# Seven half products for each gate and value panel of the first FFN, and both FFNs' inner dimension in quarters

## The chip, the cores and the metric

One core of one Trainium2 chip runs the whole program. The metric is device time in microseconds (us), the median of three runs. TensorE multiplies, ScalarE (ACT) and VectorE (DVE) do elementwise work, GpSimd (POOL) helps them, SyncE (SP) issues the loads of weights.

## The reference

Two transformer blocks with a second network behind them; the change touches the FFN of each of the two blocks (everything is float32):

```python
def swiglu(x, w_in, w_out):
    a, g = jnp.split(x @ w_in, 2, axis=-1)
    return (jax.nn.silu(a) * g) @ w_out
...
    xn = rms_norm(x, g2) * (1 + scale2) + shift2
    return x + gate2 * swiglu(xn, w_fi, w_fo)
```

`w_fi` is 1024 x 5632 (22 chunks of 128 gate columns and 22 of 128 value columns), `w_fo` is 2816 x 1024. The first block (l = 0) works on 768 tokens (512 and 256 of context), the second (l = 1) on 512. `shift`, `scale` and `gate` come from a product of `w_mod` with a conditioning vector: 96 chunks of 128 rows, the modulation chunks.

## The kernel before, in words

Activations stand with features on the partitions and tokens in the free dimension. A weight matrix is cut into panels of 128 output features; `plan()` lists them in the order in which TensorE takes them, and a panel has a running number j. A panel's product is exact to float32 by three passes of a reduced-precision format (fp32r): weight and operand are each split into a high and a low half, and high x high, high x low and low x high are added in PSUM (`panel`, L578 to L594, the matmul is L592). A panel of the first FFN's `fin` has 8 chunks x 3 passes x 2 token segments (512 and 256) = 48 matmuls, one of its `fout` 11 x 6 = 66. Results go to one of two PSUM banks in turn (`BANK`).

For panel j: SP loads it into a ring of four buffers (waiting until the low half of the panel four places before is made), ScalarE copies it to `whi` (`high`, L1132) once the panel two before is done, GpSimd subtracts to make `wlo` (L571), TensorE waits for `lo_ready`. An FFN is cut in halves: `fin{l}{half}` has 11 gate and 11 value panels in turn, `fout{l}{half}` takes the 11 hidden chunks. After a gate panel ScalarE writes silu of the bank into `fsilu` (L1424). After a value panel VectorE multiplies (`fh`, L2063, this frees the bank), ScalarE copies that to `hidden_hi` (L1429) and VectorE subtracts for `hidden_lo` (L2066, semaphore `h_lo`), which the first panel of `fout` waits for chunk by chunk. `gated_add` (L1766) adds a `fout` panel times its gate to the residual. Between these VectorE works off modulation chunks 40 to 95, one for each panel (`own_mod`, two operations over 1024 columns each, L1737), all through one buffer `modw4`: SP loads chunk k when chunk k - 1 has been worked off.

Each engine's queue is written out by hand and is executed in order; engines meet only through semaphores. While the second block's fin10 runs, VectorE also computes angles for a later stage, and ScalarE takes their sines after panel 19 of 22 (L1421). Before each norm TensorE is given some idle products (`keep_busy`, L648).

## Time and profile before

| | |
|---|---|
| median of three runs | 2265.54 us (2264.86 to 2266.88) |
| the profiled execution's own time | 2265.63 us |
| its span, first to last instruction | 2263.5 us |
| mean granted TensorE clock | 0.988 |
| busy: TensorE, VectorE, ScalarE, GpSimd | 2195.1, 1174.5, 732.7, 631.1 us |
| weight loads of TensorE (beside its matmuls) | 1775.7 us |
| matmuls | 11148 |

The profile is one execution. Busy time of an engine is the sum over its instructions; a matmul's recorded length reaches past the start of the next, so TensorE's rate is read from start to start.

### The profile page before, as it was taken

Reading aid. Unit: us, or ns where it says so; the run is one execution under the profiler, and the core shown is the slowest. Engines: PE = TensorE matmul, PEld = TensorE weight load, DVE = VectorE, ACT = ScalarE, POOL = GpSimd, SP = SyncE. Lnnn points to the kernel's source line nnn. Section 1 sums busy time; section 2 is a strip of 40 time slices with the busy share of each in tenths; the row PEclk is TensorE's granted clock in tenths of the full one; section 3 lists DMA queues with packets and bytes.
Section 4 is the critical chain, followed back from the end, with each engine's and each line's share of the span. In section 5 each row is a group of like instructions: output and inputs, shape, how many; then the busy total and the mean of one; then the engine's idle time right before and its main releaser. Section 6 shows DMA issues by size and latency. Waiting matters only on the chain.

```text
span 2263.5 us, 26814 instructions
## 1 busy us (share of the span) xinstructions
PE 2195.1 (97%) x11148; PEld 1775.7 (78%) x11148; DVE 1174.5 (52%) x1533; ACT 732.7 (32%) x1101; POOL 631.1 (28%) x272
## 2 busy tenths in 40 slices
PE   8998899999999999999999999999999999999998
PEld 6884588888888888785678888887788888888756
DVE  5987677656556665696454212347232344432172
ACT  4323424221112121424543222222263222334652
POOL 0000003223332233200144434443224444423402
PEclk9999999999999999999999999999999999989999
DMA  7302231333333342211023323323212333311301
GB/s 306 119 21 101 75 135 62 131 129 130 104 112 126 118 149 83 79 47 75 28 82 101 108 85 96 114 72 93 84 60 90 97 99 93 93 56 53 98 23 56
DMA packets 59592, 214.14 MB, mean 95 GB/s; under 512 B 6608, under 2 KB 10320, under 8 KB 58320
## 3 DMA queue, kind: packets, MB, share of 16 engines
q1 hardware_dynamic: 57024, 206.57, 27.4%
q10 hardware_dynamic: 2448, 5.85, 0.8%
q8 instruction: 89, 1.46, 0.3%
q14 instruction: 31, 0.25, 0.0%
HBM read 210.30 MB, written 2.10 MB: 94 GB/s over the span
## 4 chain that ended last, share of the span: by engine, by line
PE 89%; DVE 6%; ACT 3%; issue 1%; POOL 1%; DMA 0%; POOLq 0%; ACTq 0%; DVEq 0%
PE prod L592 74%; PE misc L638 2%; PE prod L727 1%; PE prod L807 1%; PE prod L775 1%; PE prod L862 1%; PE misc L1038 1%; PE misc L714 1%; DVE conv_acc L1941 1%; PE prod L691 1%; PE misc L886 1%; DVE stat L1872 1%; PE misc L682 1%; PE misc L874 1%; PE prod L656 1%
## 5 line engine op out<-in xcount | busy, mean ns | idle before, releaser
L571 POOL TENSOR_TENSOR wlo<-ring,whi 128x1024 fp32r<-128x1024 f32 (+3 forms) x252 | 599.4, 2379 | 1579.3 <-ACT whi L1132 1579.3
L592 PE MATMUL prod<-operand_hi,whi 128*128 128x512 f32 (+1 forms) x2080 | 769.5, 370 | 12.3 <-POOL operand_lo L558 4.6
L592 PE MATMUL prod<-operand_lo,whi 128*128 128x512 f32 (+1 forms) x2080 | 759.1, 365 | 0.0
L592 PE MATMUL prod<-operand_hi,wlo 128*128 128x512 f32 (+1 forms) x2080 | 755.6, 363 | 0.0
L1132 ACT ACTIVATE whi<-ring 128x1024 fp32r<-128x1024 f32 (+3 forms) x278 | 287.3, 1034 | 709.5 <-PE prod L592 688.1
L592 PEld LDWEIGHTS prod<-operand_hi,whi 128*128 128x128 f32 x2080 | 393.4, 189 | 90.8 <-issue 11.5
L592 PEld LDWEIGHTS prod<-operand_hi,wlo 128*128 128x128 f32 x2080 | 392.2, 189 | 64.8
L592 PEld LDWEIGHTS prod<-operand_lo,whi 128*128 128x128 f32 x2080 | 393.1, 189 | 62.9 <-issue 3.1
L592 PE MATMUL prod<-hidden_lo,whi 128*128 128x512 f32 (+1 forms) x528 | 188.0, 356 | 0.0
L592 PE MATMUL prod<-hidden_hi,whi 128*128 128x512 f32 (+1 forms) x528 | 187.6, 355 | 0.0
L592 PE MATMUL prod<-hidden_hi,wlo 128*128 128x512 f32 (+1 forms) x528 | 186.6, 353 | 0.0
L1737 DVE CUSTOM_DVE_ANT_0 mod_junk<-modw,silu_c,par 128x1024 bf16<-128x1024 f32 x68 | 121.4, 1786 | 78.8 <-DMA modw<-in_wmod 78.2
L1766 DVE SCALAR_TENSOR_TENSOR resid<-prod,par,resid 128x512 f32<-128x512 f32 x72 | 45.4, 658 | 178.2 <-PE prod L592 178.2
L2066 DVE TENSOR_TENSOR hidden_lo<-ffn_h,hidden_hi 128x768 fp32r<-128x768 f32 (+1 forms) x44 | 112.3, 2552 | 42.6 <-ACT hidden_hi L1429 42.6
L1737 DVE CUSTOM_DVE_ANT_0 modw<-modw,silu_c,par 128x1024 f32<-128x1024 f32 x68 | 132.5, 1948 | 0.0
L2063 DVE TENSOR_TENSOR ffn_h<-ffn_silu,prod 128x768 f32<-128x768 f32 (+1 forms) x44 | 36.1, 820 | 179.9 <-PE prod L592 179.9
L592 PEld LDWEIGHTS prod<-hidden_hi,whi 128*128 128x128 f32 x528 | 99.6, 189 | 15.5 <-POOL wlo L571 0.5
L592 PEld LDWEIGHTS prod<-hidden_hi,wlo 128*128 128x128 f32 x528 | 99.3, 188 | 14.7
L592 PEld LDWEIGHTS prod<-hidden_lo,whi 128*128 128x128 f32 x528 | 99.5, 188 | 13.7
L1941 DVE SCALAR_TENSOR_TENSOR conv_acc<-glu,par,conv_acc 128x798 f32<-128x798 f32 (+1 forms) x120 | 104.5, 913 | 1.3
L1424 ACT ACTIVATE ffn_silu<-prod 128x768 f32<-128x768 f32 (+1 forms) x44 | 31.0, 706 | 225.6 <-PE prod L592 225.6
L1343 ACT ACTIVATE probs_t<-misc 128x512 f32<-128x512 f32 x52 | 30.9, 595 | 66.4 <-PE misc L874 66.4
(316 smaller groups left out, 2412.1 us busy)
## 6 DMA issues: line engine op xcount, KB each, us to landing
ring<-in_w SPq DMA_DIRECT2D x224, 512.0 KB, 3.6
modw<-in_wmod SPq DMA_DIRECT2D x68, 512.0 KB, 3.6
ring<-in_w SPq DMA_DIRECT2D x32, 704.0 KB, 4.8
mod_pair<-in_wpair SPq DMA_DIRECT2D x8, 1024.0 KB, 16.8
ring<-in_wmod SPq DMA_DIRECT2D x12, 512.0 KB, 4.6
dft<-in_dftx SPq DMA_DIRECT2D x8, 512.0 KB, 5.1
resid<-in_xt SPq DMA_DIRECT2D x4, 768.0 KB, 7.6
ring<-in_w SPq DMA_DIRECT2D x12, 192.0 KB, 2.3
```

Of the source, the lines that this page charges most:

```text
L571: nc.gpsimd.tensor_tensor(wlo_of(j)[:, 0:w], ring[PLACE["panel", j] % RING][:, 0:w], whi_of(j)[:, 0:w].bitcast(F32), ALU.subtract).then_in ...
L592: mm = pe.matmul(G[b][:, t0:t0 + tn], w[:, k * P:(k + 1) * P], a[:, t0:t0 + tn], start=(i == 0 and q == 0), stop=(i == g.kc - 1 and q == 2))
L638: mm = pe.matmul(out[:, h * tb:h * tb + h], square[:, t:t + P], sel, start=(c == 0 and tb == 0), stop=(c == nchunks - 1 and tb == nb - 1), ...
L656: mm = pe.transpose(M0[:, tb * P:(tb + 1) * P], r[:, tb * P:(tb + 1) * P], ident)
L1132: nc.scalar.activation(whi_of(j)[:, 0:w], ring[PLACE["panel", j] % RING][:, 0:w], ACT.Copy).then_inc(hi_ready, 1)
L1343: nc.scalar.activation(probs_t[at % 3][:, :], M1[:, :], ACT.Copy).then_inc(pair_copied, 1)
L1424: nc.scalar.activation(fsilu[:, 0:width], src[:, 0:width], ACT.Silu).then_inc(free, 1)
L1737: nc.vector.tensor_tensor_reduce((junk, w)[s][:, 0:DC * P], w[:, 0:DC * P], silu_c[:, 1024 * s:1024 * (s + 1)], 1.0, col, ALU.mult, ALU.ad ...
L1766: ins = nc.vector.scalar_tensor_tensor(X[:, p, t0:t0 + tn], G[b][:, t0:t0 + tn], pa(f"mod{l}")[:, col:col + 1], X[:, p, t0:t0 + tn], ALU.m ...
L1941: ins = nc.vector.scalar_tensor_tensor(o, glu[:, c, tap:tap + wide], w, o, ALU.mult, ALU.add)
L2063: nc.vector.tensor_tensor(fh[:, 0:width], fsilu[:, 0:width], G[b][:, 0:width], ALU.mult).then_inc(bank_free[b], 1)
L2066: nc.vector.tensor_tensor(HL[:, p // 2, 0:width], fh[:, 0:width], HH[:, p // 2, 0:width].bitcast(F32), ALU.subtract).then_inc(h_lo, 1)
```

## The change

In the first block's FFN, after the first four panels, a gate panel and its value panel together make a unit. The 256 weight columns x 1024 features are seen as a 2 x 2 matrix of blocks (gate or value; first or second half of the features), the operand as a 2 x 2 matrix (features by halves; tokens by halves of 384), and the four result blocks come from seven products of sums of blocks (Strassen's scheme in Winograd's form) in place of eight. Each product is 4 chunks x 3 passes of 384 columns. The operand's sums are made once (`operand_sums`, `operand_sum`), the weights' sums for each unit on VectorE (`weight_sums`, `last_weight_sum`); each of the seven weight factors is split again, high on ScalarE (`half_weights`), low on VectorE for four sums (`sum_low`) and on GpSimd for the three plain blocks (`block_lows`). The results are put together in four other PSUM banks, a to d, and by VectorE's `product_sum`. Both FFNs take their 22 hidden chunks in quarters of 6, 5, 6, 5, so that there are four `fin` and four `fout` stages each and `fout` adds to the residual four times. Ring and weight buffers shrink from 11 to 8 chunks; there is one modulation chunk for each unit and for each `fout` panel, eight chunks (88 to 95, buffer `modw5`) move to the second block's `fin10`, panels 4 to 11; the angles move to `fin11`, its sines to its last panel (9). In panels whose name doesn't begin with f, the passes are the outer loop and the two token segments the inner.

The diff, cut to its core (`NTH[j]` is the number of panels up to j that are computed as before):

```diff
+PLAIN_FIRST = 4
+HALVED = {g.j0 + p for g in GEMMS if g.name[:4] == "fin0" for p in range(PLAIN_FIRST if g.name == "fin00" else 0, g.n)}
...
+def mod_places():
+    at = [GEMM["fin00"].j0 + p for p in (1, 3)]
+    for q in range(4):
+        at += [unit_panel(q, u) for u in units_of(q)]
+        at += [GEMM[f"fout0{q}"].j0 + p for p in range(8 if q < 3 else 2)]
+    return at + [GEMM["fin10"].j0 + p for p in range(4, 12)]
+MOD_AT = mod_places()
+assert len(MOD_AT) == MOD_ALL - MOD_WOUT
...
+        def weight_slot(w, q, i):
+            s, b = (i + (q > 0)) % 4, GEMM["fin00"].j0 % 2
+            return w[b if s < 2 else 1 - b][:, 512 * (s % 2):512 * (s % 2) + 512]
...
+        UB4 = M0[:, 0:HN], M0[:, 512:512 + HN], M1[:, 0:HN], MM[:, 0:HN]
...
+                if kind == "panel" and i in HALVED:
+                    q = next(q for q in range(4) if i < GEMM[f"fout0{q}"].j0)
+                    u = units_of(q)[0] + (i - unit_panel(q, units_of(q)[0])) // 2
+                    odd = (i - GEMM["fin00"].j0) % 2
+                    sp.wait_ge(w_lo, 3 * u + 2 + odd)
+                    sp.wait_ge(sum_lo, 4 * u + (1 if odd else 4))
...
-                elif j > GEMM["wout0"].j0 + 10 and own + 1 < MOD_ALL:
+                elif j == GEMM["fin00"].j0 + 3 or j - 4 in MOD_AT[:-1]:
...
+            def block_lows(q, j):
+                first = units_of(q)[0]
+                u = first + (j - unit_panel(q, first)) // 2
+                for of, at_, idx in ((0, 0, 0), (0, 512, 3), (1, 512, 6)):
+                    i = 7 * (u - first) + idx
+                    pool.wait_ge(w_hi, 7 * u + idx + 1)
+                    nc.gpsimd.tensor_tensor(weight_slot(wlo, q, i), ring[PLACE["panel", j + of] % RING][:, at_:at_ + 512],
+                                            weight_slot(whi, q, i).bitcast(F32), ALU.subtract).then_inc(w_lo, 1)
...
+                    both = [(s, x) for s in segs for x in passes] if name[0] == "f" else [(s, x) for x in passes for s in segs]
...
+            def halves(q):
+                a, b, c, d = UB4
+                first, second = slice(0, HN), slice(HN, NT)
+                steps = ((a, (XH[:, 0:4, first], XL[:, 0:4, first])), (c, (TH[1], TL[1])), (a, (TH[0], TL[0])),
+                         (b, (XH[:, 4:8, first], XL[:, 4:8, first])), (a, (XH[:, 0:4, second], XL[:, 0:4, second])),
+                         (d, (XH[:, 4:8, second], XL[:, 4:8, second])), (c, (TH[2], TL[2])))
+                for u in units_of(q):
+                    i0 = 7 * (u - units_of(q)[0])
+                    for idx, (bank, (high, low)) in enumerate(steps):
+                        if idx in (0, 3, 6):
+                            pe.wait_ge(w_lo, 3 * u + idx // 3 + 1)
+                        else:
+                            pe.wait_ge(sum_lo, 4 * u + {1: 1, 2: 2, 4: 3, 5: 4}[idx])
+                        if u == 0 and idx in (1, 2, 4, 6):
+                            pe.wait_ge(t_lo, {1: 1, 2: 2, 4: 3, 6: 4}[idx])
+                        if idx == 0:
+                            wait(pe, unit_copied, 3 * u)
+                        elif idx == 1:
+                            wait(pe, unit_sum, 4 * u)
+                        elif idx == 2:
+                            pe.wait_ge(unit_copied, 3 * u + 1)
+                        elif idx == 4:
+                            pe.wait_ge(unit_copied, 3 * u + 2)
+                        elif idx == 6:
+                            pe.wait_ge(unit_sum, 4 * u + 2)
+                        wh, wl = weight_slot(whi, q, i0 + idx), weight_slot(wlo, q, i0 + idx)
+                        for k in range(4):
+                            for t, (w, x) in enumerate(((wh, high), (wh, low), (wl, high))):
+                                mm = pe.matmul(bank, w[:, k * P:(k + 1) * P], x[:, k, :], start=(idx in (0, 1, 3, 5) and k == 0 and t == 0),
+                                               stop=(k == 3 and t == 2), skip_group_check=True)
+                        mm.then_inc(unit_done, 1)
...
                 big(f"wout{l}", xh, xl, width, begin=2)
                 rms(1, width, W, total=W[1])
-                for half in range(2):
-                    big(f"fin{l}{half}", xh, xl, width, ready=OPS[f"fin{l}0"])
-                    big(f"fout{l}{half}", lambda k: HH[:, k, :], lambda k: HL[:, k, :], width, hidden=FH * (2 * l + half + 1))
+                for q in range(4):
+                    if l or q == 0:
+                        big(f"fin{l}{q}", xh, xl, width, ready=OPS[f"fin{l}0"], panels=None if l else PLAIN_FIRST)
+                    if l == 0:
+                        halves(q)
+                    big(f"fout{l}{q}", lambda k: HH[:, k, :], lambda k: HL[:, k, :], width, hidden=CHUNKS[l, q])
...
+            def half_weights(q, i):
+                first = units_of(q)[0]
+                u, idx = first + i // 7, i % 7
+                j = unit_panel(q, u)
+                if i >= 4:
+                    act.wait_ge(unit_done, 7 * first + i - 3)
+                elif q == 0:
+                    act.wait_ge(panel_done, NTH[GEMM["fin00"].j0 + (0, 0, 3, 3)[i]])
+                else:
+                    act.wait_ge(panel_done, NTH[GEMM[f"fout0{q - 1}"].j0 + (6, 7, 7, 6)[i]])
+                gate, value = (ring[PLACE["panel", j + s] % RING] for s in range(2))
+                if idx in (0, 3, 6):
+                    landed(act, ("panel", j + (idx == 6)))
+                else:
+                    act.wait_ge(w_sum, 4 * u + {4: 1, 1: 2, 2: 3, 5: 4}[idx])
+                src = (gate[:, 0:512], value[:, 0:512], S2t[:, :], gate[:, 512:1024], S1t[:, :], gate[:, 512:1024], value[:, 512:1024])[idx]
+                nc.scalar.activation(weight_slot(whi, q, i), src, ACT.Copy).then_inc(w_hi, 1)
...
+                def hidden_half(u, half):
+                    act.wait_ge(half_ready, 2 * u + (2 if half == 0 else 1))
+                    nc.scalar.activation(HH[:, unit_chunk(q, u), HN * half:HN * half + HN], (U2t, C22t)[half][:, :],
+                                         ACT.Copy).then_inc(half_hi, 1)
+                for u in units_of(q):
+                    i0 = 7 * (u - first)
+                    for idx in range(7):
+                        act.wait_ge(unit_done, 7 * u + idx + 1)
+                        if idx == 0:
+                            wait(act, half_ready, 2 * u - 2)
+                            nc.scalar.activation(P1t[u % 2][:, :], a, ACT.Copy).then_inc(unit_copied, 1)
+                        elif idx == 2:
+                            wait(act, h_lo, CHUNKS[0, q] + unit_chunk(q, u))
+                            nc.scalar.activation(U2t[:, :], a, ACT.Copy).then_inc(unit_copied, 1)
+                        elif idx == 4:
+                            nc.scalar.activation(U4t[:, :], a, ACT.Copy).then_inc(unit_copied, 1)
+                        if i0 + idx + 4 < count:
+                            half_weights(q, i0 + idx + 4)
+                        if i0 + idx == free:
+                            high(fout)
+                        if i0 + idx == count - 1:
+                            high(fout + 1)
+                        if idx == 0 and u > first:
+                            hidden_half(u - 1, 0)
+                        elif idx == 3:
+                            act.wait_ge(unit_sum, 4 * u + 1)
+                            nc.scalar.activation(P1t[u % 2][:, :], P1t[u % 2][:, :], ACT.Silu).then_inc(unit_silu, 1)
+                        elif idx == 5:
+                            act.wait_ge(unit_sum, 4 * u + 3)
+                            nc.scalar.activation(U4t[:, :], U4t[:, :], ACT.Silu).then_inc(unit_silu, 1)
+                        elif idx == 6:
+                            hidden_half(u, 1)
+                hidden_half(u, 0)
...
+                        if g.name == "fin00" and p == 3:
+                            half_weights(0, 2)
...
+                        if g.name == "fin00" and p == 1:
+                            act.wait_ge(t_sum, 4)
+                            operand_sum(TH[1], UA[:, :, HN:NT])
+                            operand_sum(TH[0], UB[:, :, HN:NT])
+                            half_weights(0, 0)
+                            half_weights(0, 1)
+                        elif g.name == "fin00" and p == 3:
+                            half_weights(0, 3)
+                            operand_sum(XH[:, 0:4, HN:NT], UA[:, :, 0:HN])
+                            operand_sum(TH[2], UB[:, :, 0:HN])
...
+                    def next_weights(p, q=q):
+                        if p == 6:
+                            half_weights(q + 1, 0)
+                        elif p == 7:
+                            for i in (1, 2, 3):
+                                half_weights(q + 1, i)
...
+            def operand_sums():
+                dve.wait_ge(odd_lo, DC // 2)
+                dve.wait_ge(operand_lo, n["op"])
+                for U, c in ((UA, 0), (UB, 4)):
+                    ins = nc.vector.tensor_tensor(U[:, :, :], XH[:, c:c + 4, :].bitcast(F32), XL[:, c:c + 4, :].bitcast(F32), ALU.add)
+                link(ins)
+                A, B, one, two = UA, UB, slice(0, HN), slice(HN, NT)
+                for k, (o, x, y) in enumerate(((A[:, :, one], A[:, :, two], A[:, :, one]), (A[:, :, two], B[:, :, two], A[:, :, two]),
+                                               (B[:, :, two], B[:, :, two], A[:, :, one]), (B[:, :, one], B[:, :, one], B[:, :, two]))):
+                    nc.vector.tensor_tensor(o, x, y, ALU.subtract).then_inc(t_sum, 1)
+                    dve.wait_ge(t_sum, k + 1)
...
+            def weight_sums(q, u):
+                A11, _, A21, A22 = raw(q, u)
+                landed(dve, ("panel", unit_panel(q, u)))
+                landed(dve, ("panel", unit_panel(q, u) + 1))
+                wait(dve, sum_lo, 4 * (u - 1) + 3)
+                nc.vector.tensor_tensor(S1t[:, :], A21, A22, ALU.add).then_inc(w_sum, 1)
+                dve.wait_ge(w_sum, 4 * u + 1)
+                nc.vector.tensor_tensor(A21, A11, A21, ALU.subtract).then_inc(w_sum, 1)
+                nc.vector.tensor_tensor(S2t[:, :], S1t[:, :], A11, ALU.subtract).then_inc(w_sum, 1)
+            def last_weight_sum(q, u):
+                _, A12, _, _ = raw(q, u)
+                dve.wait_ge(w_lo, 3 * u + 2)
+                dve.wait_ge(w_sum, 4 * u + 3)
+                nc.vector.tensor_tensor(A12, A12, S2t[:, :], ALU.subtract).then_inc(w_sum, 1)
+            def sum_low(q, i):
+                u, idx = units_of(q)[0] + i // 7, i % 7
+                _, A12, A21, _ = raw(q, u)
...
+            def halves(q):
+                a, b, c, d = UB4
+                for u in units_of(q):
+                    i, more, k = 7 * (u - units_of(q)[0]), u < units_of(q)[-1], unit_chunk(q, u)
+                    def product_sum(which, done, copied, out, x, bank):
+                        dve.wait_ge(unit_done, 7 * u + done)
+                        dve.wait_ge(unit_copied, 3 * u + copied)
+                        nc.vector.tensor_tensor(out[:, :], x[:, :], bank, ALU.add).then_inc(unit_sum, 1)
...
+                        dve.wait_ge(unit_silu, 2 * u + silu)
+                        dve.wait_ge(unit_sum, 4 * u + (2, 4)[order])
+                        nc.vector.tensor_tensor(value[:, :], value[:, :], gate[:, :], ALU.mult).then_inc(half_ready, 1)
+                        dve.wait_ge(half_ready, 2 * u + order + 1)
+                        dve.wait_ge(half_hi, 2 * u + order + 1)
+                        o = slice(HN * half, HN * half + HN)
+                        return nc.vector.tensor_tensor(HL[:, k, o], value[:, :], HH[:, k, o].bitcast(F32), ALU.subtract)
...
+                    last_weight_sum(q, u)
+                    sum_low(q, i + 4)
+                    sum_low(q, i + 5)
+                    if more:
+                        weight_sums(q, u + 1)
+                    product_sum(1, 4, 1, P1t[u % 2], P1t[u % 2], b)
+                    mod_beside(unit_panel(q, u))
+                    if more:
+                        sum_low(q, i + 8)
+                    product_sum(2, 2, 3, C22t, U4t, c)
+                    if more:
+                        sum_low(q, i + 9)
+                    product_sum(3, 6, 3, U4t, U4t, d)
+                    product_sum(4, 7, 2, U2t, U2t, c)
+                    hidden(0, 2, C22t, U4t, 1)
+                    hidden(1, 1, U2t, P1t[u % 2], 0).then_inc(h_lo, 1)
...
+                for q in range(4):
+                    g = GEMM[f"fin{l}{q}"]
+                    if g.name == "fin00":
+                        operand_sums()
+                    for p in range(g.n if l else PLAIN_FIRST if q == 0 else 0):
+                        if g.name == "fin11" and p in (1, 4, 7):
+                            angles(p // 3)
+                        j, b = g.j0 + p, BANK[g.j0 + p]
...
+                        if g.name == "fin00" and p == 1:
+                            operand_sum_low(0, TL[1], UA[:, :, HN:NT], TH[1])
+                            operand_sum_low(1, TL[0], UB[:, :, HN:NT], TH[0])
+                            weight_sums(0, 0)
+                            sum_low(0, 1)
+                        elif g.name == "fin00" and p == 3:
+                            sum_low(0, 2)
+                            operand_sum_low(2, XL[:, 0:4, HN:NT], UA[:, :, 0:HN], XH[:, 0:4, HN:NT])
+                            dve.wait_ge(h_lo, 2)
+                            operand_sum_low(3, TL[2], UB[:, :, 0:HN], TH[2])
+                        mod_beside(j)
...
+                    def beside_fout(p, l=l, q=q):
+                        if l == 0 and q < 3 and p == 5:
+                            weight_sums(q + 1, units_of(q + 1)[0])
+                        elif l == 0 and q < 3 and p == 7:
+                            sum_low(q + 1, 1)
+                            sum_low(q + 1, 2)
+                        mod_beside(GEMM[f"fout{l}{q}"].j0 + p)
```

## Rows read from the trace of the kernel before

**Rows 1.** The page's chain that ended last, share of the span by engine.

```profile
PE 89%; DVE 6%; ACT 3%; issue 1%; POOL 1%; DMA 0%; POOLq 0%; ACTq 0%; DVEq 0%
```

**Rows 2.** Chain in order of time: start us, us, what; both FFNs.

```profile
364.96 553.62 PE prod L592 x3162
...
1161.97 358.84 PE prod L592 x1581
```

**Rows 3.** Windows over both FFNs: us, each engine's busy us, clock, DMA share, GB/s.

```profile
365.00:918.50 553.50, 553.50 (x3163) 484.54 (x3164) 328.77 (x318) 113.42 (x125) 173.24 (x62) 1.00 0.33 115
1162.00:1520.50 358.50, 358.50 (x1581) 296.61 (x1582) 118.72 (x89) 99.69 (x120) 158.89 (x62) 1.00 0.30 97
```

**Rows 4.** Timeline, first FFN, TensorE: start us, us, engine, line, operation.

```profile
799.75 0.40 PE L592 MATMUL prod<-operand_hi,whi 128*128 128x512 f32 x1
...
800.45 0.28 PE L592 MATMUL prod<-operand_hi,whi 128*128 128x256 f32 x1
...
800.80 0.40 PE L592 MATMUL prod<-operand_hi,whi 128*128 128x512 f32 x1
```

**Rows 5.** Timeline around a short wait of TensorE at a panel's end.

```profile
1118.95 0.39 PE L592 MATMUL prod<-operand_hi,wlo 128*128 128x512 f32 x1
...
1119.38 1.06 ACT L1132 ACTIVATE whi<-ring 128x1024 fp32r<-128x1024 f32 x1 [1.82 <-PE prod L592]
...
1119.56 0.50 PE L592 MATMUL prod<-operand_hi,whi 128*128 128x512 f32 x1 [0.22 <-POOL wlo L571]
...
1119.90 0.40 PE L592 MATMUL prod<-operand_lo,whi 128*128 128x512 f32 x1
```

**Rows 6.** Timeline, first FFN, VectorE, GpSimd and ScalarE.

```profile
642.46 1.27 DVE L1737 CUSTOM_DVE_ANT_0 mod_junk<-modw,silu_c,par 128x1024 bf16<-128x1024 f32 x1
...
642.54 3.45 POOL L571 TENSOR_TENSOR wlo<-ring,whi 128x1024 fp32r<-128x1024 f32 x1 [8.10 <-ACT whi L1132]
...
643.66 3.42 DVE L1737 CUSTOM_DVE_ANT_0 modw<-modw,silu_c,par 128x1024 f32<-128x1024 f32 x1
...
650.84 1.28 DVE L1737 CUSTOM_DVE_ANT_0 mod_junk<-modw,silu_c,par 128x1024 bf16<-128x1024 f32 x1 [3.75 <-DMA modw<-in_wmod]
...
659.19 0.85 ACT L1429 ACTIVATE hidden_hi<-ffn_h 128x768 fp32r<-128x768 f32 x1
...
659.34 2.40 POOL L571 TENSOR_TENSOR wlo<-ring,whi 128x1024 fp32r<-128x1024 f32 x1 [4.96 <-ACT whi L1132]
...
660.07 2.48 DVE L2066 TENSOR_TENSOR hidden_lo<-ffn_h,hidden_hi 128x768 fp32r<-128x768 f32 x1 [0.91 <-ACT hidden_hi L1429]
```

**Rows 7.** Groups by line and form: count, busy us, mean ns, idle before.

```profile
L1624 DVE TENSOR_TENSOR wlo<-ring,whi 128x1024 fp32r<-128x1024 f32 x26 | 31.8, 1221 | 12.6 <-ACT whi L1132 12.4
...
L1730 DVE TENSOR_TENSOR proj<-proj,work 128x512 f32<-128x512 f32 x8 | 5.5, 692 | 0.3
...
L2140 DVE TENSOR_TENSOR ce_u<-prod,ce_c 128x512 f32<-128x512 f32 x8 | 5.5, 692 | 37.9 <-PE prod L592 37.9
...
L1803 DVE TENSOR_REDUCE stat<-prod 128x1 f32<-128x384 f32 x8 | 4.1, 551 | 0.1
...
L1429 ACT ACTIVATE hidden_hi<-ffn_h 128x512 fp32r<-128x512 f32 x22 | 13.5, 613 | 0.0
...
L1132 ACT ACTIVATE whi<-ring 128x384 fp32r<-128x384 f32 x12 | 6.3, 524 | 0.0
...
L558 POOL TENSOR_TENSOR operand_lo<-work,operand_hi 128x512 fp32r<-128x512 f32 x4 | 5.2, 1292 | 4.0 <-ACT work L1192 4.0
```

**Rows 8.** Windows of 10 us between stages, columns as in rows 3.

```profile
350.00:360.00 10.00, 7.77 (x37) 6.56 (x37) 4.66 (x11) 4.66 (x7) 2.35 (x1) 0.83 0.00 0
1160.00:1170.00 10.00, 8.96 (x38) 7.17 (x39) 6.47 (x10) 7.83 (x11) 6.36 (x5) 1.00 0.25 79
```

**Rows 9.** Timeline, GpSimd, start of the first FFN.

```profile
373.63 2.28 POOL L558 TENSOR_TENSOR operand_lo<-work,operand_hi 128x768 fp32r<-128x768 f32 x1 [1.57 <-ACT work L1192]
```

**Rows 10.** Timeline, ScalarE, the sine operations in the second FFN.

```profile
1270.42 0.63 ACT L1421 ACTIVATE sinT<-angles 128x512 f32<-128x512 f32 x1 [3.89 <-PE prod L592]
```

211 lines of the change are left out of this document (135 added, 76 removed).

## The prediction

> **What bounds the kernel now.** I read the page's chain first: TensorE carries 89% of it [rows 1]. Then the chain in order of time: the first layer's FFN is one unbroken run of matmuls of 553.6 us, the second layer's another of 358.8 us [rows 2]. The stage windows say the same: TensorE is busy for the whole of both stretches at granted clock 1.00, while VectorE is busy for 328.8 of 553.5 us, GpSimd for 173.2, ScalarE for 113.4 [rows 3]. So nothing waits in front of TensorE there, work taken from it is time gained, and anything that makes it wait is time lost in full.
>
> Its rate: six matmuls, three of 512 and three of 256 columns, take 1.05 us [rows 4], 0.175 us each. In the second layer 1581 matmuls of 512 columns take 358.8 us [rows 2], 0.2267 each. A line through 0.2267 at 512 and the 0.1233 that is left for 256 gives 0.175 for 384 columns, the new width. By columns alone at the 512 rate it would be 0.170: the lower bound. By columns at the 256 form's rate it would be 0.185: the upper bound. I take 0.175, as 384 lies midway. (At 0.170 the queues below give 6 us less; at 0.185 some 10 us more, as part of it comes out of the waits.)
>
> **The gain.** A unit (gate and value panel of one chunk) was 96 matmuls, 16.80 us. Strassen's is 7 products x 4 x 3 = 84 matmuls of 384 columns, 14.70 us, 2.10 for a product. Twenty units: -42.0 us. The fout matmuls (1056) and the four plain panels (192) stay. The FFN would take 512.4 us in place of 554.4.
>
> The Trainium skill (TensorE: Matmul & The Clock Gate, Back-to-back issue gap) puts a matmul of N columns at N/2.4 ns plus 2.5, 0.1625 us for 384; twenty units would then be 21 us shorter still. By that rule a 512-column one is 0.216, and the trace, with 0.2267, does not agree, so the sum goes by the trace.
>
> **What each product now waits for.** Prices of one operation: VectorE tensor_tensor of 512 0.69, whether both sources are in SBUF or one in PSUM; of 1024 1.22; of 384 0.55; ScalarE 384 0.52, 512 0.61; GpSimd 512 1.29 [rows 7]. So VectorE's 1536-wide sums are 1.75 and the 3072-wide 3.35 (0.53 for each further 512). A modulation chunk is two operations of 1.27, 1.20 from start to start [rows 6]. A product's end is seen by the other engines 0.20 after its last slot, and a TensorE that had to wait starts at once but loses 0.1 on its first matmul [rows 5].
>
> VectorE and GpSimd shut each other out when VectorE reads two SBUF tensors: at 642.54 GpSimd's 2.40 us operation waits for VectorE's and lasts 3.45; the modulation half that follows waits for it in turn, 3.42 in place of 1.27; at 660.07 a 0.95 us subtraction takes 2.48 beside GpSimd's [rows 6]. Before, TensorE had 8.4 us a panel to hide this. The Trainium skill (SBUF — State Buffer, Who interferes with whom) calls it an exclusive lock, taken for a whole instruction by whoever comes first, and leaves out VectorE operations with one SBUF input; the trace agrees (3.45, 3.42). That rule speaks against the change, since all weight sums and their low parts read two SBUF tensors; without it the sum would be the first rival's, below.
>
> The rest comes from going through the five instruction queues of the diff in order, each operation starting when its engine and its semaphores allow, at these prices (a semaphore costs 0.04: hidden_hi ends at 660.04, its reader starts at 660.07 [rows 6]). In a middle unit, counted from its first matmul: product 3 ends at 8.40, and VectorE, free since 8.2, starts its sum at 8.62, to 9.17. The first modulation half runs 9.10 to 10.37. ScalarE has meanwhile made the next unit's first high half (8.62 + 0.62 = 9.24), and GpSimd asks for the port at 9.28, gets it at 10.3 and holds it to 11.60. The second half ends at 12.74, the low part of the next unit's product 1 at 13.3, and the sum that empties bank c (product_sum 2) at 13.8. Product 6 adds into that bank and was due at 12.60: **1.2 us of waiting, with the restart 1.3, in each unit**. A unit is 16.0, not 14.7.
>
> *Middle units*: the last unit of a quarter has no next sums and no such wait, the first has its own (below); 2 + 3 + 4 + 3 = 12 are left, 12 x 1.3 = 15.7.
>
> *Start.* operand_sums puts 2 x 3.35 + 4 x 1.75 = 13.7 us on VectorE behind the norm. It starts once GpSimd's last odd low half (begun at 373.63 [rows 9], 9.5 after the stage's start: 3168 slots of 0.175 back from the end of its run in [rows 2], 918.58) and the plain low half behind it are through, at 13.5; a further 2.2 go to GpSimd. VectorE reaches panel 1's hidden product at 29.3; panel 3, due at 25.2, needs its bank: 5.1 lost. Then come the four splits of 1536 on both engines: product 2 of the first unit waits 4.8 (bank a's copy is behind two splits on ScalarE), product 4 1.6 (its copy is behind a high half that needs A12's sum, behind panel 3's modulation chunk), product 6 3.8 (1.2 as above, and two GpSimd halves of 1.29 among the next unit's sums). With restarts 15.7.
>
> *First units of quarters 1 to 3.* The modulation chunk of the last fout panel lies in front of their sums: product 6 waits 1.2 + 2.47 = 3.6 each, with restarts 11.2. Product 1 waits 0.4, 7.7, 0.4: a chunk needs 3.75 for its DMA after the one before [rows 6], one buffer, and 2.47 on VectorE, 6.2 in all, against a fout panel of 36 x 0.175 = 6.30 us (six chunks) or 5.25 (five). After the five-chunk fout of quarter 1 VectorE is 8 x 1 us behind. With restarts 8.8.
>
> *fout panels*: short waits for the last hidden chunk (2 x 0.5), a bank (0.65), a low half (0.86): 3.0 with restarts.
>
> First layer: 512.4 + 15.7 + 15.7 + 11.2 + 8.8 + 3.0 = 566.8, +12.4 against before.
>
> **Second layer.** Its matmuls are the same. Eight modulation chunks now sit behind fin10's panels 4 to 11, where a panel is 24 x 0.2267 = 5.44 us: 6.2 each, plus 1 to 2 where GpSimd's 2.40 falls in between. They slip behind the panels: a bank is late by 0.6, the last hidden chunk of the first fout by 5.3, another bank by 1.7. At each of the four quarter ends the last hidden chunk has only 3.4 or 2.7 us (5 or 4 chunks x 3 x 0.2267) where it had 6.8: 0.4, 0.1, 0.4, and a low half 0.3. The two Sin operations, 0.63 each [rows 10], a little overlapped, move to the last panel of a quarter, ahead of its hidden chunk: 1.1, with nothing to hide them. With restarts 10.3. More gated adds (16 more panels x 0.75) lie in VectorE's idle time (118.7 busy of 358.5 [rows 3]); were it full they would cost 12.
>
> **Clock.** One 10 us window in which TensorE is busy for 7.8 us has a granted clock of 0.83; one with 8.96 keeps 1.00 [rows 8]. The 1.2 us waits in 16 are of the second kind. Four waits above 4 us (5.1, 4.8, 7.7, 5.3) could each lose up to 1.7 us; I take half, as TensorE is not the bound just then: 3.4. Bounds 0 and 13.6 (all eight waits above 3 us).
>
> **Other edits.** The new order of passes for panels outside the FFN keeps all matmuls and weight loads of each panel: 0, bounds -3 and +3 (504 slots of 512 columns in the first layer, 0.0066 each: by recorded starts such a slot is 0.233 in the mix [rows 4], 0.2267 alone). The smaller ring, the sixth modulation buffer and the addresses: 0, as landing (3.75 after the request) stays shorter than a unit; if a ring slot came late, the next unit's sums would be late and it would add to product 6's wait.
>
> **Sum.** -42.0 + 54.4 + 10.3 + 3.4 = +26.1. The profiled execution took 2265.6 us, the median of the runs is the same 2265.5: **2291.7 us**, 1.2% slower.
>
> **Rivals.**
> 1. *The port is free when it counts* (other side: faster). Without GpSimd's 1.28 between the modulation halves, VectorE needs 0.22 + 0.49 + 1.20 + 1.20 + 0.62 + 0.55 = 4.3 us from product 3's end to the emptying of bank c, and has 4.2: the wait is 0.1 and the units fall to 15.0 or so with their round trips. The same queues without any shutting-out give 539.3 for the first layer and +3.8 for the second: 2265.6 - 15.1 + 3.8 = 2254.3. It decides when GpSimd's request comes over 1.2 us later, after the second half has started. Against it: [rows 6] show the collision whenever the two meet. 0.17.
> 2. *TensorE stays the bound*: 2265.6 - 42.0 + 2 for the quarter ends = 2226. For it: VectorE's own work in a unit is 8 x 0.69 + 8 x 0.55 + 2.5 = 12.4 us of 14.7. Against: it must come in a fixed order between products. 0.05.
> 3. *A worse phase*: GpSimd's low half of product 6 asks for the port 0.03 us after the last weight sum took it. If it comes first, everything behind is 0.8 later in 12 units: 2301. 0.12, with the clock's upper bound (2302) inside it.
> 4. *In between*: partly hidden start, 0.170 a slot (-6), no clock loss: some 2261 to 2270, no measurable change. 0.08.
>
> My forecast has 0.58, own range 2275 to 2300. The range is 2254 to 2310, which leaves the second rival, the lower half of the first and a tail above outside. 0.2% (4.5 us) is about what can be told from no change. Faster 0.22, same 0.08, slower 0.70.
>
> **What would show it.** Right: a matmul slot of 0.175 in the products; a wait of TensorE once a unit, ended by VectorE's sum into value_late, with a unit period near 16.0; first FFN near 567 us; a gap of some 5 us in front of the sixth chunk of fout10's first panel, ended by hidden_lo; modulation halves of 2.5 to 3.4 us. Wrong if the period is at 14.7 to 15.2, if the start costs under 8 us, or if the clock falls below 0.9 through whole quarters.

## The result and the profile after

The changed kernel takes 2304.81 us (2303.35 to 2308.41), beside 2266.21 us (2264.86 to 2269.34) for the kernel before on the same chip, medians of four runs each: ratio 1.0171, 95% interval 1.0153 to 1.0188. It is slower, by 1.7%; the prediction said 1.2% (2291.7 us, range 2254 to 2310). The profiled execution has a span of 2302.3 us, 38.8 more than before's 2263.5.

The page's chain, share of the span by engine and by line:

```profile
PE 55%; DVE 7%; issue 4%; ACT 3%; DMA 2%; POOL 1%; POOLq 0%; DVEq 0%; ACTq 0%; SPq 0%
PE prod L699 41%; DMA modw<-in_wmod 2%; PE misc L764 2%; PE prod L764 2%; PE prod L872 1%; PE misc L783 1%; DVE mod_junk L1974 1%; DVE modw L1974 1%; PE misc L1186 1%; PE misc L859 1%; PE prod L836 1%; PE prod L952 1%; POOL wlo L675 1%; DVE conv_acc L2272 1%; PE misc L793 1%
```

Before, TensorE carried 89% of it [rows 1]. Now the transfer of modulation chunks and the two operations on them (L1974) stand in it: these are what was hidden before. The windows over both FFNs, and over the stretches behind three long waits (columns as in [rows 3]):

```profile
362.45:942.30 579.85, 526.40 (x2923) 492.08 (x2924) 423.44 (x608) 202.20 (x346) 161.38 (x98) 0.97 0.31 102
1188.68:1559.27 370.59, 362.99 (x1581) 298.44 (x1582) 138.31 (x137) 103.99 (x136) 163.18 (x78) 0.99 0.33 102
...
412.50:416.50 4.00, 4.00 (x16) 4.00 (x16) 3.83 (x8) 1.53 (x3) 0.00 (x0) 0.63 0.30 108
668.00:672.00 4.00, 4.00 (x15) 4.00 (x15) 3.82 (x7) 0.63 (x1) 0.00 (x0) 0.56 0.30 84
1263.30:1267.50 4.20, 4.20 (x11) 3.23 (x11) 3.05 (x3) 0.84 (x1) 1.82 (x1) 0.50 0.83 313
```

TensorE is idle for 53 us of the first FFN, where before it had no gap [rows 3]; VectorE's busy time went from 329 to 423 us. And behind a long wait the granted clock is at half speed for some three to six microseconds (0.50 to 0.63 in windows that take in its end).

A middle unit, VectorE, GpSimd and the matmuls that matter (timeline; start us, us, then what; in brackets idle time and what ended it):

```profile
705.12 0.33 PE L764 MATMUL prod<-operand_hi,whi 128*128 128x384 f32 x1
...
706.40 1.50 POOL L658 TENSOR_TENSOR wlo<-ring,whi 128x512 fp32r<-128x512 f32 x1 [5.16 <-ACT whi L1317]
...
706.67 1.78 DVE L2051 TENSOR_TENSOR weight_sum<-weight_sum,ring 128x512 f32<-128x512 f32 x1
...
707.20 0.33 PE L764 MATMUL prod<-operand_hi,whi 128*128 128x384 f32 x1
...
708.15 1.45 POOL L658 TENSOR_TENSOR wlo<-ring,whi 128x512 fp32r<-128x512 f32 x1 [0.25 <-ACT whi L1317]
...
708.38 0.54 DVE L2077 TENSOR_TENSOR first_product<-first_product,prod 128x384 f32<-128x384 f32 x1
...
708.84 1.85 DVE L1974 CUSTOM_DVE_ANT_0 mod_junk<-modw,silu_c,par 128x1024 bf16<-128x1024 f32 x1
...
710.62 1.28 DVE L1974 CUSTOM_DVE_ANT_0 modw<-modw,silu_c,par 128x1024 f32<-128x1024 f32 x1
...
711.83 0.68 DVE L2067 TENSOR_TENSOR wlo<-ring,whi 128x512 fp32r<-128x512 f32 x1
...
712.43 0.54 DVE L2077 TENSOR_TENSOR value_late<-sum_four,misc 128x384 f32<-128x384 f32 x1
...
713.12 0.41 PE L764 MATMUL misc<-sum_hi,whi 128*128 128x384 f32 x1 [1.59 <-DVE value_late L2077]
```

The first and the fourth row give a product: 12 slots (a slot is from the start of a matmul to the start of the next) in 2.08 us, 0.1733 each. Product 3 ended in time (707.2), but the last weight sum took 1.78 instead of 0.69, because GpSimd was at the port, so its sum began at 708.38; then the first modulation half took 1.85 beside GpSimd's second low half, then the second half, the low half, and bank c was free at 712.97, 1.6 us after TensorE wanted it. Note 708.38: this sum has one input in PSUM, and takes its plain 0.54 beside GpSimd's 1.45. The Trainium skill (SBUF — State Buffer, Who interferes with whom) says that a VectorE instruction with at most one SBUF input, outside the two-port modes, does not contend with GpSimd; the trace agrees with 0.54. The period of the middle units is 16.39 to 16.43 us.

Two of the long waits, with TensorE's first slots behind them (third quarter's first unit; fout10's first panel):

```profile
665.97 0.69 PE L764 MATMUL misc<-sum_hi,whi 128*128 128x384 f32 x1 [8.42 <-DVE wlo L2067]
666.46 0.52 PE L764 MATMUL misc<-sum_lo,whi 128*128 128x384 f32 x1
666.78 0.52 PE L764 MATMUL misc<-sum_hi,wlo 128*128 128x384 f32 x1
...
1262.98 0.80 PE L699 MATMUL prod<-hidden_hi,whi 128*128 128x512 f32 x1 [5.19 <-DVE hidden_lo L2397]
1263.58 0.63 PE L699 MATMUL prod<-hidden_lo,whi 128*128 128x512 f32 x1
1264.01 0.63 PE L699 MATMUL prod<-hidden_hi,wlo 128*128 128x512 f32 x1
```

A slot of 384 columns is 0.32 us here instead of 0.1735, one of 512 is 0.43 instead of 0.2267, until 671.3 and 1268.7. What VectorE did ahead of the second of them:

```profile
1258.44 1.29 DVE L1974 CUSTOM_DVE_ANT_0 mod_junk<-modw,silu_c,par 128x1024 bf16<-128x1024 f32 x1 [3.82 <-DMA modw<-in_wmod]
...
1260.86 0.68 DVE L2394 TENSOR_TENSOR ffn_h<-ffn_silu,prod 128x512 f32<-128x512 f32 x1
1262.24 0.69 DVE L2397 TENSOR_TENSOR hidden_lo<-ffn_h,hidden_hi 128x512 fp32r<-128x512 f32 x1 [0.69 <-ACT hidden_hi L1645]
```

It stood still for 3.82 us for a chunk's transfer, with the hidden chunk that TensorE needed queued behind it.

**Where the 38.8 us are.** A stage runs here from TensorE's start behind GpSimd's last odd low half to the end of its last fout matmul, in the profiled executions:

| kernel | first FFN | between | second FFN |
|---|---|---|---|
| before | 553.6 | 243.4 | 358.8 |
| after | 580.0 | 246.2 | 370.8 |
| mod_after_sum3 | 589.7 | 243.6 | 370.8 |
| tiny_mods | 534.4 | 245.3 | 362.0 |
| tiny_pool_lows | 554.9 | 243.5 | 370.8 |
| two_late | 580.5 | 243.6 | 362.1 |
| quarters_alone | 557.3 | 243.5 | 362.1 |
| pass_order_alone | 553.6 | 245.1 | 358.8 |
| sum2_first | 552.8 | 244.9 | 370.6 |
| all_three | 549.5 | 251.2 | 362.0 |
| two_buffers | 543.7 | 245.8 | 361.2 |
| three_of_eight | 534.9 | 245.6 | 361.0 |
| light_start | 531.3 | 248.6 | 361.1 |

So +26.4 in the first FFN and +11.9 in the second. The stages ahead of the first FFN end between 359.8 and 367.7 us and the middle is 243.4 to 246.2 in kernels with the same code there, so after's -2.5 and +2.8 in these are no effect of the change. Each row is one execution; that of two_buffers was some 5 us faster than the median of its runs (2255.4 against 2260.2).

### The profile page after: what moved, and what is told of

Same layout as the page of the kernel before. It is cut to its first block, busy times and chain, and to the rows that moved or that the text cites. A ratio compares the mean times of both kernels' runs of the same rounds, so it can differ in the third digit from the quotient of the medians.

```text
span 2302.3 us, 27623 instructions
## 1 busy us (share of the span) xinstructions
PE 2173.3 (94%) x10908; PEld 1784.6 (78%) x10908; DVE 1289.6 (56%) x1871; ACT 825.7 (36%) x1337; POOL 623.8 (27%) x324
## 4 chain that ended last, share of the span: by engine, by line
PE 55%; DVE 7%; issue 4%; ACT 3%; DMA 2%; POOL 1%; POOLq 0%; DVEq 0%; ACTq 0%; SPq 0%
PE prod L699 41%; DMA modw<-in_wmod 2%; PE misc L764 2%; PE prod L764 2%; PE prod L872 1%; PE misc L783 1%; DVE mod_junk L1974 1%; DVE modw L1974 1%; PE misc L1186 1%; PE misc L859 1%; PE prod L836 1%; PE prod L952 1%; POOL wlo L675 1%; DVE conv_acc L2272 1%; PE misc L793 1%
## 5 line engine op out<-in xcount | busy, mean ns | idle before, releaser
L675 POOL TENSOR_TENSOR wlo<-ring,whi 128x1024 fp32r<-128x1024 f32 (+4 forms) x244 | 503.1, 2062 | 1338.8 <-ACT whi L1280 1338.8
L699 PE MATMUL prod<-operand_hi,whi 128*128 128x512 f32 (+1 forms) x1440 | 522.9, 384 | 17.1 <-DVE ffn_h L2394 5.9
L699 PE MATMUL prod<-operand_lo,whi 128*128 128x512 f32 (+1 forms) x1440 | 510.5, 375 | 0.0
L699 PE MATMUL prod<-operand_hi,wlo 128*128 128x512 f32 (+1 forms) x1440 | 510.3, 375 | 0.0
L1280 ACT ACTIVATE whi<-ring 128x1024 fp32r<-128x1024 f32 (+4 forms) x270 | 251.6, 932 | 534.2 <-PE prod L699 507.7
L699 PEld LDWEIGHTS prod<-operand_hi,whi 128*128 128x128 f32 x1440 | 258.5, 189 | 80.4 <-issue 16.0
L699 PEld LDWEIGHTS prod<-operand_lo,whi 128*128 128x128 f32 x1440 | 258.6, 189 | 49.5 <-issue 2.2
L699 PEld LDWEIGHTS prod<-operand_hi,wlo 128*128 128x128 f32 x1440 | 258.3, 189 | 49.6
L658 POOL TENSOR_TENSOR wlo<-ring,whi 128x512 fp32r<-128x512 f32 x60 | 90.5, 1510 | 284.8 <-ACT whi L1317 284.8
L1974 DVE CUSTOM_DVE_ANT_0 mod_junk<-modw,silu_c,par 128x1024 bf16<-128x1024 f32 x68 | 100.9, 1484 | 49.5 <-DMA modw<-in_wmod 48.9
L1317 ACT ACTIVATE whi<-ring 128x512 fp32r<-128x512 f32 x100 | 62.9, 629 | 120.8 <-DVE ring L2058 50.7
L1974 DVE CUSTOM_DVE_ANT_0 modw<-modw,silu_c,par 128x1024 f32<-128x1024 f32 x68 | 95.1, 1399 | 0.0
```

The source lines that it names most:

```text
L658: nc.gpsimd.tensor_tensor(weight_slot(wlo, q, i), ring[PLACE["panel", j + of] % RING][:, at_:at_ + 512], weight_slot(whi, q, i).bitcast(F3 ...
L675: nc.gpsimd.tensor_tensor(wlo_of(j)[:, 0:w], ring[PLACE["panel", j] % RING][:, 0:w], whi_of(j)[:, 0:w].bitcast(F32), ALU.subtract).then_in ...
L699: mm = pe.matmul(G[b][:, t0:t0 + tn], w[:, k * P:(k + 1) * P], a[:, t0:t0 + tn], start=(i == 0 and q == 0), stop=(i == g.kc - 1 and q == 2))
L1280: nc.scalar.activation(whi_of(j)[:, 0:w], ring[PLACE["panel", j] % RING][:, 0:w], ACT.Copy).then_inc(hi_ready, 1)
L1317: nc.scalar.activation(weight_slot(whi, q, i), src, ACT.Copy).then_inc(w_hi, 1)
L1974: nc.vector.tensor_tensor_reduce((junk, w)[s][:, 0:DC * P], w[:, 0:DC * P], silu_c[:, 1024 * s:1024 * (s + 1)], 1.0, col, ALU.mult, ALU.ad ...
```

## The experiments

The kernels are edits of the changed kernel, but for quarters_alone and pass_order_alone, which start from the kernel before. Ratios are to the kernel before, measured beside each on the same chip; its medians there were 2266.2 to 2269.1 us, so that times of different experiments compare to some 3 us. The text counts a unit's products from 0 to 6, as the code does; where an expectation speaks of a fifth or third product, of a copy of product 5's bank or of products 3, 5 and 7, it counts from 1.

**mod_after_sum3.** The chunk of a unit behind product_sum 3.

```diff
                     product_sum(1, 4, 1, P1t[u % 2], P1t[u % 2], b)
-                    mod_beside(unit_panel(q, u))
...
                     product_sum(3, 6, 3, U4t, U4t, d)
+                    mod_beside(unit_panel(q, u))
```

> The modulation chunk of a unit stands behind product_sum 3 instead of product_sum 1. Theory A (VectorE's fixed order puts the chunk's two halves between product 3's end and the emptying of bank c): the 1.59 us wait in front of product 6 goes in all twelve middle units, their period falls from 16.4 to 14.6-14.8 us, product 6 of the four first units waits 2 to 3 us less each; some 25 us in all, 2275 to 2282 us. Theory B (what delays product 6 is the weight sums and low halves shut out by GpSimd, the chunk only fills the time): the wait stays at 1 us or more, under 8 us gained, 2297 or more. Theory C: the chunk collides in its new place and product 2 of the next unit waits instead: period 15.5 or more.

Measured: 2315.72 us, ratio 1.0218 (1.0191 to 1.0245), slower than the changed kernel. None of the three theories had this. In front of product 6 of the middle units the waits are now 0.3 us in four and 2.3 to 2.5 us in eight. One of the good ones:

```profile
713.66 1.40 POOL L658 TENSOR_TENSOR wlo<-ring,whi 128x512 fp32r<-128x512 f32 x1 [5.79 <-ACT whi L1317]
...
713.83 1.78 DVE L2051 TENSOR_TENSOR weight_sum<-weight_sum,ring 128x512 f32<-128x512 f32 x1
...
715.53 0.54 DVE L2077 TENSOR_TENSOR first_product<-first_product,prod 128x384 f32<-128x384 f32 x1
...
716.10 0.53 ACT L1355 ACTIVATE first_product<-first_product 128x384 f32<-128x384 f32 x1 [0.77 <-DVE first_product L2077]
...
716.73 0.49 ACT L1344 ACTIVATE sum_four<-prod 128x384 f32<-128x384 f32 x1
...
717.12 0.62 ACT L1317 ACTIVATE whi<-ring 128x512 fp32r<-128x512 f32 x1
...
717.78 0.69 DVE L2067 TENSOR_TENSOR wlo<-ring,whi 128x512 fp32r<-128x512 f32 x1 [1.71 <-ACT whi L1317]
...
718.39 0.55 DVE L2077 TENSOR_TENSOR value_late<-sum_four,misc 128x384 f32<-128x384 f32 x1
```

VectorE is idle for 1.71 us where the chunk was, and the bank is emptied only 1.2 us earlier, not by the chunk's 2.5: from the start of product_sum 1 to that of product_sum 2 it is 2.86 us (4.05 in the changed kernel), for product_sum 1 lets ScalarE's Silu go, behind which stand the copy of product 4's bank, a high half, its low half on VectorE, and only then product_sum 2. The chunk had filled this round trip. In the units with the long wait, two weight sums in place of one are shut out by GpSimd:

```profile
695.80 1.66 DVE L2050 TENSOR_TENSOR ring<-ring,ring 128x512 f32<-128x512 f32 x1
...
697.38 1.77 DVE L2051 TENSOR_TENSOR weight_sum<-weight_sum,ring 128x512 f32<-128x512 f32 x1
...
702.40 0.41 PE L764 MATMUL misc<-sum_hi,whi 128*128 128x384 f32 x1 [2.51 <-DVE value_late L2077]
```

Behind four of these longer waits the slots are too long by 1.6 us in sum, and the first fout panel of a quarter waits 1.2 to 1.6 us instead of 0.8 or less: the chunk in its new place makes the last hidden chunk later. Together that is some 11 us, of which shorter waits in the first units give a part back: the first FFN is 9.7 us longer. My "VectorE idle here, so there is room there" looked at one engine only.

**tiny_mods.** Chunks 40 to 95 on 8 of 1024 columns, which leaves out that part of the modulation.

```diff
+                n_ = 8 if k >= MOD_WOUT else DC * P
...
-                    nc.vector.tensor_tensor_reduce((junk, w)[s][:, 0:DC * P], w[:, 0:DC * P], silu_c[:, 1024 * s:1024 * (s + 1)],
+                    nc.vector.tensor_tensor_reduce((junk, w)[s][:, 0:n_], w[:, 0:n_], silu_c[:, 1024 * s:1024 * s + n_],
```

> The 56 modulation chunks from the first FFN on (40 to 95) work on 8 of their 1024 columns, so that work is left out and the output is not the reference's. Theory A: middle units at 14.6-14.8 us, no wait for the low half in front of product 1 of the first units (8.4 and 2 x 1.6 gone), product 6 of the first units waits 1.3 us or less, the 5.2 and 1.3 us waits in fin10 and the first fout of the second layer go; of 66 us of waits some 12 are left (start and short ones), and the half-clock slots mostly go: 2235 to 2248 us. If the weight sums and GpSimd's low halves alone fill VectorE (theory B), half of the waits stay: 2265 or more.

Measured: 2251.87 us, ratio 0.9933 (0.9909 to 0.9957), 53 us under the changed kernel (expected 57 to 70). The units' period is 15.13, the waits in front of the quarters' product 1 and the 5.2 and 0.6 us waits of the second layer are gone; the start (5.3, 1.5 and 3.0 us) and 0.30 in each unit stay.

**tiny_pool_lows.** GpSimd's low halves on 8 of 512 columns, which leaves out the rest of these low parts.

```diff
-                    nc.gpsimd.tensor_tensor(weight_slot(wlo, q, i), ring[PLACE["panel", j + of] % RING][:, at_:at_ + 512],
+                    nc.gpsimd.tensor_tensor(weight_slot(wlo, q, i)[:, 0:8], ring[PLACE["panel", j + of] % RING][:, at_:at_ + 8],
```

> GpSimd's three low halves of a unit work on 8 of 512 columns (the rest of these low parts is left as it was, so the products are not exact). Modulation chunk where it was. Theory A with the port as its second half: the last weight sum and the first modulation half no longer wait for GpSimd (1.78 and 1.85 become 0.7 and 1.28), 1.6 us less between product 3 and the emptying of bank c: period 14.7-15.0 us, 2275 to 2285. Without any shutting-out between the two engines (rival): the period stays at 16.4 and the time within 3 us of 2305.

Measured: 2277.54 us, ratio 1.0049 (1.0032 to 1.0066), as theory A had it. The same place in a unit, weight sum and first modulation half at their plain lengths:

```profile
676.05 0.69 DVE L2051 TENSOR_TENSOR weight_sum<-weight_sum,ring 128x512 f32<-128x512 f32 x1
...
677.35 1.28 DVE L1974 CUSTOM_DVE_ANT_0 mod_junk<-modw,silu_c,par 128x1024 bf16<-128x1024 f32 x1
...
681.31 0.41 PE L764 MATMUL misc<-sum_hi,whi 128*128 128x384 f32 x1 [0.30 <-DVE value_late L2077]
```

Period 15.13. Either of the two, the chunk or GpSimd at the port, is enough to remove the 1.6 us wait; it takes both to make it. The 0.30 that is left is the round trip.

**two_late.** Two buffers in turn for the eight chunks behind fin10's panels, the second in the place of the sums' tiles.

```diff
-                own = (k - MOD_RING) % 4 if k < MOD_WOUT else 4 + (k >= MOD_LATE)
+                own = (k - MOD_RING) % 4 if k < MOD_WOUT else 4 if k < MOD_LATE else 5 + k % 2
...
+                elif k > MOD_LATE:
+                    sp.wait_ge(mod_step, mods_done(k - 2))
```

> The eight chunks behind fin10's panels use two buffers in turn. Theory A (one buffer: 3.75 us of DMA and 2.5 us on VectorE in series, 6.2 against a panel of 5.4, make the hidden chunks late): the 5.2 us wait before the sixth chunk of the first fout and the 1.3 us bank wait behind it go, with the half-clock slots behind them: 7 to 9 us, 2296 to 2298. Rival (VectorE's and GpSimd's time in fin10, not the transfer, is what is too long): 3 us gained or less.

Measured: 2299.54 us, ratio 1.0145 (1.0126 to 1.0165); the second FFN 362.1 us, 8.7 less. The 5.2 us wait, its half-speed slots and the bank's wait are gone. The median is only 5.3 us lower, outside the 7 to 9 that were expected: the stages ahead of the first FFN, which have the same code, took 5 us more in the profiled execution (they end at 367.7 against 362.5).

**quarters_alone and pass_order_alone.** The kernel before with only its inner dimension in quarters, and with only the new order of passes.

```diff
-            (f"fin{l}0", 8, 2 * FH), (f"fout{l}0", FH, 8),
-            (f"fin{l}1", 8, 2 * FH), (f"fout{l}1", FH, 8))]
+            *(x for q in range(4) for x in ((f"fin{l}{q}", 8, 2 * QUARTER[q]), (f"fout{l}{q}", QUARTER[q], 8))))]
```

> The kernel before with its inner dimension in quarters of 6, 5, 6, 5 chunks in both FFNs, one modulation chunk a panel from the first panel on as before, no Strassen, old order of passes. By the prediction's steps: quarter ends 0.4, 0.1, 0.4, a low half 0.3, the Sin operations 1.1 in the second layer, with restarts about 3 us; nothing in the first, whose hidden chunk has 4.2 us or more: 2 to 4 us over the kernel before. Rival (the second layer's 11.9 us are mostly the quarters'): 8 us or more.

> The kernel before with only the new order of passes outside the FFNs (passes outside, segments inside). Predicted 0, bounds -3 and +3. If the 2.5 us that the stages ahead of the first FFN are shorter come from the order, they are shorter here too, and the slot of a 512 and 256 pair is measurably different; if they do not, those stages take what they took before to 0.5 us.

Measured: quarters 2275.26 us, ratio 1.0040 (1.0025 to 1.0055): some 8 us by the medians, twice what was expected, 6.9 by the stages. The rival is wrong all the same, since only 3.2 us are in the second FFN, half of them at the end of the second quarter, where the Sin operations are (in two_buffers, which moves them, this wait is 0.31):

```profile
1319.60 0.50 PE L593 MATMUL prod<-hidden_hi,whi 128*128 128x512 f32 x1 [1.33 <-DVE hidden_lo L2074]
```

and 3.7 are in the first, which I had at nothing: three fout panels of the second quarter (5.25 us each) wait 0.55 to 0.93 us for VectorE's gated add, and the panel behind them waits 0.63. The changed kernel has one such wait (0.67). Order of passes: 2268.09 us, ratio 1.0000 (0.9989 to 1.0012), both FFNs the same to 0.1 us. It costs nothing that these runs can tell (the interval is some 2.5 us to each side). The stages ahead of the first FFN end at 364.3 us, 365.0 before.

**sum2_first.** What mod_after_sum3 taught, in VectorE's queue and in ScalarE's.

```diff
+            def weight_sums(q, u, between=lambda: None):
...
+                between()
                 nc.vector.tensor_tensor(S2t[:, :], S1t[:, :], A11, ALU.subtract).then_inc(w_sum, 1)
...
+                        weight_sums(q, u + 1, product_sum_1)
...
+                    product_sum(2, 2, 3, C22t, U4t, c)
+                    mod_beside(unit_panel(q, u), 0)
                     if more:
                         sum_low(q, i + 8)
                         sum_low(q, i + 9)
                     product_sum(3, 6, 3, U4t, U4t, d)
+                    mod_beside(unit_panel(q, u), 1)
                     product_sum(4, 7, 2, U2t, U2t, c)
...
-                        elif idx == 3:
+                        elif idx == 4:
                             act.wait_ge(unit_sum, 4 * u + 1)
```

> VectorE's order in a unit: product_sum 1 between the second and the third weight sum of the next unit, product_sum 2 (which empties bank c) right behind, then the modulation chunk's first half, the two low halves, product_sum 3, the second half; ScalarE's first Silu behind the copy of product 5's bank instead of in front of it. The theory that the first run shaped (bank c must be emptied within one product of 2.08 us after product 5; the round trip copy, Silu, high half, low half and the chunk each stand in front of that sum): nothing of the chunk or of the ScalarE round trip is left in front, period 14.6-14.8 us in the middle units against 16.4, product 6 of first units waits 1.5 us or more less, the waits of product 1 (chunks late behind the fout panels) stay; 2272 to 2282 us. Rival: VectorE is simply full (some 13.5 us of work in 14.6 with the waits for the port), the period stays at 15.5 or more and the time over 2290.

Measured: 2280.52 us, ratio 1.0065 (1.0048 to 1.0082), 24 us under the changed kernel. The time is in the expected range, the period is not: it is 15.18 and not 14.6 to 14.8. Bank c is now free in time to 0.1, but the chunk's second half makes product_sum 4 late, for which the next unit's product 1 waits 0.3. In the profile:

```profile
691.49 1.67 DVE L2050 TENSOR_TENSOR ring<-ring,ring 128x512 f32<-128x512 f32 x1
693.09 0.54 DVE L2078 TENSOR_TENSOR first_product<-first_product,prod 128x384 f32<-128x384 f32 x1
693.55 1.31 DVE L2052 TENSOR_TENSOR weight_sum<-weight_sum,ring 128x512 f32<-128x512 f32 x1
694.79 0.54 DVE L2078 TENSOR_TENSOR value_late<-sum_four,misc 128x384 f32<-128x384 f32 x1
```

GpSimd shuts VectorE out as often as before (1.67 and 1.31 for 0.69); the sum that TensorE waits for is only no longer behind the rest. In front of the first fout panel of three quarters the waits grew to 1.6 us, from 0.5 to 0.8 in the changed kernel.

**all_three.** sum2_first, two_late, and 7, 6, 7, 6 chunks behind the fout panels of the quarters.

> sum2_first, two buffers for the chunks behind fin10, and 7, 6, 7, 6 chunks behind the fout panels of the four quarters in place of 8, 8, 8, 2 (so the last panel of a quarter has none). Product 1 of the third quarter waits 3 us or less instead of 8.4, product 6 of the first units 1 us or less; the 5.2 us wait of the second layer is gone: 2260 to 2269 us, about the kernel before. Left are the start (some 10 us), what remains in the first fout of the second layer and half-clock slots.

Measured: 2275.64 us, ratio 1.0038 (1.0025 to 1.0051). The third quarter's product 1 waits 3.3 us instead of 8.4, but six chunks in the last quarter make VectorE late for its gated adds (1.1 and 1.9 us) and for the norm behind, which costs some 6 us ("between", 251.2). It is 6.6 us over the expected range: moving the chunks moves the wait.

**two_buffers and three_of_eight.** A second buffer for chunks beside fout panels, on top of sum2_first and two_late; the last unit of a quarter keeps VectorE's old order, and the Sin operations move to fin12.

```diff
+        at.append(5 + k % 2 if k >= MOD_LATE else 7 if name[:4] == "fout" and p % 2 else 4)
...
+                            if u == first and q:
+                                act.wait_ge(mod_step, mods_done(MOD_WOUT + MOD_AT.index(fout - 2 * QUARTER[q] - 1)))
```

> sum2_first and the two buffers behind fin10, and for the first layer's FFN a second modulation buffer for every other fout panel (in the place of the product tiles, which are free between units), chunk places as in the changed kernel (8, 8, 8, 2); in the last unit of a quarter VectorE keeps the old order; the two Sin operations are moved on to fin12's fourth panel. Theory (the 8.4 us wait of the third quarter's first product is transfer and VectorE time in series in one buffer): that wait falls to 2 us or less, the half-clock slots behind it go, hidden chunks of the first fout panels wait 0.5 us again instead of 1.6, the second layer's 1.3 us wait goes: some 12 us under sum2_first for the first layer and 7 to 9 for the second, 2254 to 2262 us, 0.2 to 0.5% under the kernel before. Rival (VectorE is behind by its own work in these quarters, not by the transfer): 4 us or more of that wait stay, 2264 or more.

Measured: 2260.24 us, ratio 0.9964 (0.9951 to 0.9976), the first version faster than the kernel before. Product 1 of the third quarter no longer waits: the 8.4 us were the transfer in series with VectorE's work, not VectorE's work. A new wait of 2.4 us came in each of three quarters, for ScalarE's first copy, since the buffer lies in the product tiles (two of the three have 1.6 us of half-speed slots behind them, one has none):

```profile
522.92 0.41 PE L794 MATMUL prod<-sum_hi,whi 128*128 128x384 f32 x1 [2.38 <-ACT first_product L1370]
```

In three_of_eight the second buffer serves panels 2, 4 and 6, so it is free a panel earlier.

> two_buffers showed a new wait of 2.4 us in front of the third product of each quarter's first unit: ScalarE may copy its bank only when VectorE is done with the chunk of the last fout panel, which lies in the place of the product tile. Here the second buffer is used for the fout panels 2, 4 and 6 instead of 1, 3, 5 and 7. Theory: the three waits of 2.4 us (with the half-clock slots behind two of them, 0.9 to 1.6 us) are gone or under 0.5: 6 to 10 us less, 2250 to 2256 us, if the chunks still keep pace; rival: the chunk of panel 7 is then late in its one buffer and product 2 waits instead, 2258 or more.

Measured: 2248.73 us, ratio 0.9913 (0.9888 to 0.9938). All three waits are gone. Its two FFNs, columns as in [rows 3]:

```profile
361.93:896.81 534.88, 521.46 (x2923) 482.16 (x2924) 443.62 (x608) 195.48 (x346) 160.50 (x98) 0.99 0.33 111
1142.41:1503.45 361.04, 360.17 (x1582) 296.62 (x1583) 143.63 (x137) 104.07 (x136) 164.42 (x78) 1.00 0.34 105
```

**light_start.** No chunks beside fin00's panels, four beside the last fout's.

> three_of_eight without the modulation chunks beside fin00's second and fourth panel; the last quarter's fout panels carry four in place of two. Theory (VectorE is the bound from the norm to the second unit: 13.7 us of sums of operands, four low parts of 1.75, weight sums, two chunks of 2.5): the 5.3 us wait for panel 3's bank stays, since it is ahead of both chunks; the 2.7, 0.5 and 0.4 us waits in front of products 3, 5 and 7 of the first unit shrink by 3 us or more in all: 2246 to 2253 us. Rival (ScalarE's four splits of 1536 make these waits): they stay, and the two chunks more in the last quarter cost 1 to 2 us.

Measured: 2248.57 us, ratio 0.9912 (0.9896 to 0.9928), the same as three_of_eight. The three waits of the first unit fell from 4.5 to 1.8 us, so VectorE's load makes most of them; but the stretch behind the last fout, with two chunks more in front of it, is 3 us longer (248.6 against 245.6; kernels with equal code there differ by up to 2.8, so how much of it the chunks cost is open). The wait for panel 3's bank is 3.8 here and 5.3 there, and it takes either value in kernels with the same code in that place; the point on the half-speed slots below says why.

## Why the prediction came out as it did

Direction and mechanisms were right; the time was 13 us low. Counted by the slots as recorded, the term for the clock was 10 us too small and the waits of the first layer 5 us. That the waits agree so well is in part luck, as the point on the half-speed slots shows.

- **The gain**: 0.1735 a slot against 0.175, so 84 slots are 14.57 us and 1680 of them 291.5: 2.5 us better than taken. (The 0.1233 for 256 columns is not what [rows 4] show, which is 0.117 beside 0.233 for 512; the line through these gives 0.175 too. The 0.55 for a sum of 384 columns was read from a reduction in [rows 7]; the sums took 0.54.)
- **Middle units** (1.3 us each, 15.7): right in place, in cause and in the bank; 12 units wait 1.48 to 1.60 us, and 0.17 more from start to start (the profile counts idle time from a matmul's recorded end, which lies that much behind its slot), 20.9. The order at the port was the third rival's: GpSimd's low half got in ahead of the last weight sum (1.78). It then no longer fell between the modulation halves but over the first one (1.85). Together a unit has 1.85 us over its slots where the forecast had 1.3: 0.5 more and not the rival's 0.8.
- **Start** (15.7): 5.3, 3.3 and 3.5 us, from start to start 12.6. Product 4's 1.6 did not come.
- **First units**: product 6 waits 3.80, 1.08 and 3.55, from start to start 8.9 (predicted 11.2); product 1 1.62, 8.42 and 1.62, 12.2 (8.8). **fout panels** 2.9 (3.0).
- Together the waits are 57.6 us, and 59.7 with what the first slot behind each is too long by (0.08 to 0.11, the prediction's restart), against 54.4 predicted: low by 9%. It is that close by luck, since some 6.5 us of half-speed slots stand where waits would be (below).
- **Second layer** (10.3): 0.55, 5.19, 1.33, 0.22 and 0.31, from start to start 8.4, with the first slots 8.9; the second bank wait of 1.7 did not come, and the Sin operations are in the 1.33. quarters_alone puts 3.2 on the quarters, two_late 8.7 on the single buffer, and 358.8 + 3.2 + 8.7 = 370.7 is the measured stage.
- **Clock** (3.4, bounds 0 and 13.6): the step with the largest error. I took half of 1.7 us for each of four waits. The first FFN less its slots (291.5 + 1248 x 0.175 = 509.9) and its waits (57.6) leaves 12.5 us, the second less 358.8 and 8.4 leaves 3.5: 16 in all. Some 2.6 of it are the first slots. Seven waits are 3.3 us or more, and the slots behind each of them are too long by 1.4 to 2.8 us in sum, 13.6 us together without the first slots' usual 0.1; behind 1.6 us and less only the first slot is. The step priced the loss from windows [rows 8] and not from slots behind a wait, and counted four waits where seven were long enough. It is 10.2 us off. With the gain (-2.5), the waits of the first layer (+5.3) and of the second (-1.4) this gives the miss of 12.7 (38.8 measured, 26.1 predicted) to 1.1 us.
- **What the half-speed slots cost.** I halved the loss because TensorE is not the bound just then, and that argument holds for three of the seven waits: there the slow slots only use up time that TensorE would have waited for VectorE and ScalarE.

  From the stage's start to the release of panel 3's bank it is 29.7 us in all ten kernels with products in units: where the slots in it are too long by 1.6 us the wait is 3.8, where they are not it is 5.3. From there to product 2 it is 17.4 us in seven kernels, with 1.4 us of slow slots and a wait of 3.3 in the changed kernel, with 2.7 and 1.9 in three_of_eight.

  From product 2 to product 6 it is 14.80 here and 14.79 in two_late, whose slow slots there are 1.1 us less; product 4 has no wait here, 0.5 there and 2.1 in three_of_eight, which has no slow slots there.

  Product 6 of the third quarter's first unit starts 14.3 us behind product 1, as in the second (14.5) and fourth (14.3) quarters, though the slots between are too long by 2.6 us: its wait is shorter by as much.

  So of the 13.6 us about 6.5 were taken out of the next wait and about 7 made the kernel longer, half as the prediction had it, but of a far larger sum. At full clock throughout, the waits of the first layer would have been some 66 us (59.7 + 6.5, an estimate from the above) and not 54.4: seen by causes, the clock's term was short by some 4 us and the queues by some 12, of these 0.5 in each of 12 middle units and 3.4 in front of product 1.

The wait for panel 3's bank in sum2_first, whose stage starts at 363.57, behind slow slots:

```profile
393.30 0.47 PE L699 MATMUL prod<-operand_hi,whi 128*128 128x512 f32 x1 [3.76 <-DVE ffn_h L2397]
```

The same wait in the changed kernel (stage start 362.45), and product 6 of the first units of the second and the third quarter:

```profile
392.17 0.77 PE L699 MATMUL prod<-operand_hi,whi 128*128 128x512 f32 x1 [5.31 <-DVE ffn_h L2394]
...
544.12 0.41 PE L764 MATMUL misc<-sum_hi,whi 128*128 128x384 f32 x1 [3.80 <-DVE value_late L2077]
...
680.27 0.41 PE L764 MATMUL misc<-sum_hi,whi 128*128 128x384 f32 x1 [1.08 <-DVE value_late L2077]
```

- **Other edits** at 0: confirmed for the order of passes (1.0000).
- **Rival 1** (2254): tiny_pool_lows shows what it was about. With the port free the units fall to 15.13, as it said, but the first FFN only to 554.9 and not to its 539.3: the waits of 5.3 us at the start and of 8.4 in the third quarter, and the half-speed slots, are still there. **Rival 2** (TensorE the bound) is not met even by three_of_eight, whose first FFN is 534.9 where TensorE's own time is 509.9.

That the scheme loses is then not in the products but in what stands around them. With the queues reordered and the chunks given a second buffer, the same scheme is 0.9% faster than the kernel before. Of the 25 us that the first FFN of three_of_eight still has over its matmuls, 12.6 are waits that the profile names, 10.4 of them at the start; most of the rest is 0.6 us in each unit (period 15.18 against 14.57), which no kernel here took away, and 2.7 us of half-speed slots behind its one wait of 5.3.

## To carry to other kernels

Where matrix work is replaced by additions on another engine, price the sum that frees a bank by everything queued in front of it on every engine of its round trip, and put it first; an idle gap on one engine is no room if another's chain runs through it. Work that was hidden (here the modulation chunks) must be re-costed against the shorter cover, transfer and compute in series if it has one buffer: 6.2 us against panels of 5.25 and 5.44 made 8.4 and 5.2 us waits, and a second buffer removed both. Behind every wait of TensorE as long as the seven here (3.3 us and more) put 1.4 to 2.8 us of half-speed slots into the queue model, and let it find out whether the next wait takes them up; adding them to the sum is right only where no such wait follows.

## What the runs showed of the hardware

Behind the changed kernel's waits of 3.3 to 8.4 us the granted clock of TensorE was at its half level for 2.5 to 6 us (0.32 us a slot of 384 columns, 0.43 of 512); in some at once (behind 8.42, 5.31, 5.19, 3.55, 3.28), in others only after 1.1 to 1.5 us at full speed (behind 3.80 and 3.50). In the FFNs of the other kernels every wait of 3.3 us and more has such slots too; waits between 1.8 and 3.1 us have them in some places and not in others (mod_after_sum3: 2.51 with 1.6 us, 2.50 with none; tiny_pool_lows: 1.81 with 1.7, 1.83 with none); behind those of 1.7 us and less there are none, but for the 1.4 us wait at the very start of the first FFN, which has 1.6 us of such slots in four kernels. Behind the first FFN the kernel before has a wait of 1.74 us with 1.7 us of them, and behind the second one of 1.75 with none. The first slot behind any wait is 0.08 to 0.11 us too long. A fp32r matmul of 384 columns takes 0.1735 us back to back, of 512 0.2267, at full granted clock. A GpSimd operation of only 8 columns still took 0.30 us, and 1.05 us beside a modulation half.
